# A streaming RWKV-7 and latent-attention layer: the chunk stage with one 64x64 step matrix per chunk and batched products

## The reference

```python
def step(S, inp):                     # S: (heads, 64 values, 64 keys)
    r_t, w_t, k_t, v_t, kk_t, a_t = inp
    sa = jnp.einsum('bhvk,bhk->bhv', S, kk_t)
    S = (S * w_t[:, :, None, :] + v_t[..., None] * k_t[:, :, None, :]
         - sa[..., None] * (kk_t * a_t)[:, :, None, :])
    return S, jnp.einsum('bhvk,bhk->bhv', S, r_t)
```

## Time and profile before

| | |
|---|---|
| time, median of 3 runs | 2530.11 us (2524.06 to 2531.42) |
| the profiled execution's own time | 2529.77 us |
| its span | 2528.1 us |
| mean granted TensorE clock | 0.988 |
| TensorE busy, of the span | 2453.5 us, 97% |
| TensorE weight loads | 2245.9 us, 89% |
| VectorE | 1140.8 us, 45% |
| ScalarE | 861.8 us, 34% |
| GpSimd | 108.6 us, 4% |
| DMA moved | 284.10 MB, mean 112 GB/s |

### The profile page before, as it was taken

One profiled execution on the slowest core, in us unless ns is written; L12 is line 12 of the kernel. 1 busy time (PEld: TensorE's weight loads), 2 busy tenths in 40 slices (PEclk: granted clock), 3 DMA queues, 4 the chain that ended last, 5 costly groups with the idle time before them and its releaser, 6 DMA issues.

```text
span 2528.1 us, 43507 instructions
## 1 busy us (share of the span) xinstructions
PE 2453.5 (97%) x17004; PEld 2245.9 (89%) x17004; DVE 1140.8 (45%) x1840; ACT 861.8 (34%) x1295; POOL 108.6 (4%) x182
## 2 busy tenths in 40 slices
PE   6999999999999999999999899999999999999997
PEld 6888888888889999999978899999878999999886
DVE  4566665665433333344433544444332444444234
ACT  4433333333333322344323433333222333333232
POOL 4000000000010000000000000000000000000010
PEclk9999999999999999999999999999999999999999
DMA  5322222222443433244544344444444444444443
GB/s 161 106 74 72 66 69 70 79 74 73 116 118 108 117 93 99 86 123 126 166 125 125 92 126 129 127 124 124 125 125 124 125 125 127 129 126 134 136 126 128
DMA packets 414536, 284.10 MB, mean 112 GB/s; under 512 B 31728, under 2 KB 392690, under 8 KB 413536
## 3 DMA queue, kind: packets, MB, share of 16 engines
q1 hardware_dynamic: 405600, 259.16, 35.0%
q0 software_dynamic: 8832, 23.36, 3.3%
HBM read 275.55 MB, written 6.92 MB: 112 GB/s over the span
## 4 chain that ended last, share of the span: by engine, by line
PE 94%; DVE 3%; issue 1%; ACT 1%; DMA 1%; POOL 0%; DVEq 0%; SPq 0%; POOLq 0%; ACTq 0%
PE banks L1419 20%; PE banks L869 19%; PE banks L873 18%; PE banks L870 18%; PE banks L320 2%; PE banks L882 2%; PE banks L883 2%; PE banks L884 2%; PE banks L384 1%; PE banks L1282 1%; PE banks L446 1%; PE banks L1285 1%; PE banks L440 1%; PE banks L1380 1%; PE banks L457 0%
## 5 line engine op out<-in xcount | busy, mean ns | idle before, releaser
L859 DVE TENSOR_TENSOR w_lo<-w_raw,w_hi 128x1024 fp32r<-128x1024 f32 x482 | 590.3, 1225 | 970.5 <-ACT w_hi L854 969.2
L869 PE MATMUL banks<-x_hi,w_hi 128*128 128x384 f32 x2640 | 917.5, 348 | 8.2 <-DVE w_lo L859 8.2
L873 PE MATMUL banks<-x_hi,w_lo 128*128 128x384 f32 x2640 | 887.5, 336 | 0.0
L870 PE MATMUL banks<-x_lo,w_hi 128*128 128x384 f32 x2640 | 886.4, 336 | 0.0
L854 ACT ACTIVATE w_hi<-w_raw 128x1024 fp32r<-128x1024 f32 x482 | 511.3, 1061 | 1042.4 <-PE banks L873 599.4
L869 PEld LDWEIGHTS banks<-x_hi,w_hi 128*128 128x128 f32 x2640 | 498.6, 189 | 29.0 <-DVE w_lo L859 10.1
L870 PEld LDWEIGHTS banks<-x_lo,w_hi 128*128 128x128 f32 x2640 | 498.4, 189 | 4.9 <-issue 0.2
L873 PEld LDWEIGHTS banks<-x_hi,w_lo 128*128 128x128 f32 x2640 | 498.2, 189 | 1.2 <-issue 1.2
L1419 PE MATMUL banks<-w_hi,act_hi 128*128 128x512 f32 x528 | 163.6, 391 | 4.6 <-DVE h_rows L1976 2.4
L1419 PE MATMUL banks<-w_hi,act_lo 128*128 128x512 f32 x528 | 164.2, 392 | 0.0
L1419 PE MATMUL banks<-w_lo,act_hi 128*128 128x512 f32 x528 | 163.8, 392 | 0.0
(11 more groups left out here) (395 smaller groups left out, 2395.1 us busy)
## 6 DMA issues: line engine op xcount, KB each, us to landing
w_raw<-in_w_ffn_in SPq DMA_DIRECT2D x176, 512.0 KB, 3.8
w_raw<-in_w_in SPq DMA_DIRECT2D x144, 512.0 KB, 3.8
w_raw<-in_w_ffn_down SPq DMA_DIRECT2D x88, 512.0 KB, 3.6
w_raw<-in_w_out SPq DMA_DIRECT2D x32, 512.0 KB, 3.6
w_raw<-in_w_o_a SPq DMA_DIRECT2D x16, 512.0 KB, 4.0
w_raw<-in_w_o_b SPq DMA_DIRECT2D x16, 512.0 KB, 3.9
w_raw<-in_w_in SPq DMA_DIRECT2D x20, 256.0 KB, 3.7
w_ukv_head<-in_w_ukv POOLq DMA_DIRECT2D x8, 512.0 KB, 4.0
```

The lines of the kernel that those rows point to most:

```text
L859: nc.vector.tensor_tensor(lo[:, s], raw[:, s], hi[:, s].bitcast(F32), ALU.subtract).then_inc(lo_done, 1)
L869: nc.tensor.matmul(out, hi[:, s, k, :], xh[:, kt, :], start=kt == 0, stop=False)
L870: nc.tensor.matmul(out, hi[:, s, k, :], xl[:, kt, :], start=False, stop=False)
L873: last = nc.tensor.matmul(out, lo[:, s, k, :], xh[:, kt, :], start=False, stop=kt == 15)
```

## The change

r and u of all chunks are made before any state is known, in batches. `m_t` v is taken in level 4, for all chunks and the samples, into bank 7, and ScalarE copies it to `ra[:, 0:3]`. In the front four more products turn alpha to token-major form, `ra[:, 3:5]`. One group then multiplies `t_f` with both (128 columns per product): u without the state, and the decayed alpha matrix; a second set of products makes the latter's transposed form `p_t`. The gain of each chunk's state and a 64x64 matrix per chunk and head (`step_made`, to which VectorE adds the identity: `s_step`) follow for all four chunks together. The states are then stepped three times by `s_step`, one product per head and chunk, added in the bank to the gain; `next_state` scales the sum by two columns at once. Afterwards `p_t` times the incoming states corrects u for all chunks in one subtraction, and the output is summed for two chunks per product (128 columns).

The samples' spread `vx` has four blocks of 64 columns in place of eight; the two halves of the tokens (partitions 0 to 63 and 64 to 127) hold four sequences each, so the update takes four products per source, 64 rows by 64 columns of weights with 256 columns, one in each quarter of the array, and values and u are summed in the bank. One addition to the states is left of two. The constant mask shrinks from 8 to 4 columns.

One piece moves from the run after the third `pieces(2)` into the chunk stage, which has six in place of five.

```diff
@@ constants, tiles
-NC2 = R2 + NT + 8
+NC2 = R2 + NT + 4
...
+        ra = region("r_and_alpha", [P, 5, P])
+        un_s = t_y[:, 0:2, :].rearrange("p i c -> p (i c)")
+        u_and_p = region("u_and_p_neg", [P, 2, 2, P])
+        p_t = region("decayed_alpha_t", [P, 2 * P])
+        s_step = t_x[:, 0:4, :].rearrange("p (h t) c -> p h t c", h=2)
+        s_in = region("state_in", [P, 4, 64])
...
+        state_sum = lambda c, r=slice(0, P): ps[r, 2 + 2 * (c % 2), 64 * (c // 2):64 * (c // 2) + 64]
+        step_made = lambda c, r=slice(0, P): ps[r, 2 + 2 * (c % 2), 128 + 64 * (c // 2):192 + 64 * (c // 2)]
+        by_half = [(t, p, i) for t in range(2) for i in range(2) for p in range(2)]
+        by_parity = [(t, p, i) for t in range(2) for p in range(2) for i in range(2)]
@@ pe_rwkv, front
+            for t in range(2):
+                for i in range(2):
+                    last = mm_(ps[:, 2 + i, 384 + 64 * t:448 + 64 * t], al[heads(i), i, tile_tok(t)],
+                               ident[heads(i), heads(i)], start=True, stop=True)
             last.then_inc(E("tok_ps"), 1)
@@ pe_rwkv, levels
                 last.then_inc(E("g_ps"), 1)
+                if lv == 4:
+                    for t, p, i in by_half:
+                        mm_(ps[heads(p), 7, 128 * t + 64 * i:128 * t + 64 * i + 64], m_t[heads(p), 3 * i + t, heads(p)],
+                            v[heads(p), t, heads(i)], start=True, stop=True)
+                    mm_(ps[:, 7, 256:384], asd[:, :], ident, start=True, stop=False, skip_group_check=True)
+                    for i in range(2):
+                        last = mm_(ps[:, 7, 256 + 64 * i:320 + 64 * i], m_t[:, 3 * i + 2, :], v[:, 2, heads(i)],
+                                   start=False, stop=True, skip_group_check=True)
+                    last.then_inc(E("r_ps"), 1)
                 pieces(1, level_ready)
...
+                if b == 6:
+                    pe.wait_ge(E("r_done"), f + 1)
@@ pe_rwkv, chunk stage (the loop over c goes)
+            pe.wait_ge(E("c_done"), f * 2 + 2)
+            wp = ps[:, 2, :].rearrange("p (t q c) -> p t q c", t=2, q=2)
+            for t, p, i in by_half:
+                last = mm_(wp[heads(p), t, :, heads(i)], t_f[heads(p), 3 * i + t, heads(p)], ra[heads(p), t:t + 4:3, heads(i)],
+                           start=True, stop=True)
+            last.then_inc(E("u_ps"), 1)
+            for i in range(2):
+                last = mm_(ps[:, 3, heads(i)], t_f[:, 3 * i + 2, :], ra[:, 2, heads(i)], start=True, stop=True)
+            last.then_inc(E("u_ps"), 1)
+            for t, p, i in by_parity:
+                last = mm_(ps[heads(i), 6 + p, 64 * t:64 * t + 64], ra[heads(p), 3 + t, heads(i)],
+                           t_f[heads(p), 3 * i + t, heads(p)], start=True, stop=True)
+            last.then_inc(E("u_ps"), 1)
+            pieces(1)
+            pe.wait_ge(E("u_done"), f * 2 + 2)
+            pe.wait_ge(E("pa_done"), f + 1)
+            for t, p, i in by_parity:
+                r = heads(p)
+                mm_(state_sum(2 * t + p, heads(i)), tok[r, 0, t, heads(i)], v[r, t, heads(i)],
+                    start=t == 0, stop=False, skip_group_check=True)
+            for t, p, i in by_parity:
+                r = heads(p)
+                mm_(state_sum(2 * t + p, heads(i)), tok[r, 1, t, heads(i)], u_and_p[r, t, 0, heads(i)],
+                    start=False, stop=True, skip_group_check=True)
+            for t, p, i in by_parity:
+                r = heads(p)
+                last = mm_(step_made(2 * t + p, heads(i)), u_and_p[r, t, 1, heads(i)], tok[r, 1, t, heads(i)],
+                           start=False, stop=True, skip_group_check=True)
+            last.then_inc(E("state_ps"), 1)
...
+            pieces(1)
+            for c in range(1, 4):
+                pe.wait_ge(E("state_done"), f * 4 + c)
                 for i in range(2):
+                    last = mm_(state_sum(c, heads(i)), s_step[heads(i), c % 2, c // 2, :], s_in[heads(i), c, :],
+                               start=False, stop=True, skip_group_check=True)
                 last.then_inc(E("state_ps"), 1)
+                if c < 3:
                     pe.wait_ge(E("vx_done"), f * 2 + c)
                     for i in range(2):
+                        for r in range(2):
+                            last = mm_(ps[heads(i), 6 + r, 0:256], tok[heads(r), c - 1, 2, heads(i)],
+                                       vx[heads(r), i].rearrange("p b v -> p (b v)"), start=c == 1, stop=c == 2)
                     last.then_inc(E("sd_ps"), 1)
+                    pieces(1)
+            for t, p, i in by_parity:
+                last = mm_(ps[heads(p), 2 + i, 256 + 64 * t:320 + 64 * t], p_t[heads(i), 128 * t + 64 * p:128 * t + 64 * p + 64],
+                           s_in[heads(i), 2 * t + p, :], start=True, stop=True)
+            last.then_inc(E("us_ps"), 1)
...
+            pieces(1)
+            pe.wait_ge(E("us_done"), f + 1)
...
             pieces(1)
...
-            pieces(4)
+            pieces(3)
@@ act_rwkv
+            fn(ra[:, 3:5, :].rearrange("p t (i c) -> p i t c", i=2),
+               ps[:, 2:4, 384:512].rearrange("p i (t c) -> p i t c", t=2), ACT.Copy).then_inc(E("alpha_done"), 1)
             cut(0)
...
+            act.wait_ge(E("r_ps"), f + 1)
+            fn(ra[:, 0:3, :], ps[:, 7, 0:NT], ACT.Copy).then_inc(E("r_done"), 1)
             cut(3)
...
+            act.wait_ge(E("u_ps"), f * 3 + 1)
+            fn(u_and_p[:, :, :, :].rearrange("p t q c -> p (t q c)"), ps[:, 2, :], ACT.Copy, scale=-1.0).then_inc(E("u_done"), 1)
+            act.wait_ge(E("u_ps"), f * 3 + 2)
+            fn(un_s[:, :], ps[:, 3, 0:P], ACT.Copy, scale=-1.0).then_inc(E("u_done"), 1)
@@ dve_rwkv, chunk stage
+            def next_state(c):
+                return nc.vector.tensor_scalar(s_in[:, c + 1, :], state_sum(c), e1[:, 64 * c + 63:64 * c + 64],
+                                               emid[:, c + 1, 0:1], M, M)
+            dve.wait_ge(E("u_ps"), f * 3 + 3)
+            cp(p_t[:, :].rearrange("p (t h c) -> p h t c", t=2, h=2),
+               ps[:, 6:8, 0:128].rearrange("p h (t c) -> p h t c", t=2)).then_inc(E("pa_done"), 1)
+            dve.wait_ge(E("tok_done"), f + 1)
+            by_sequence(tok[:, 2, 2, :])
+            if more:
+                dve_scan(f + 1, ch)
+            dve.wait_ge(E("state_ps"), f * 4 + 1)
+            next_state(0)
+            tt(s_step[:, :, :, :], each(fold["ident"], 2),
+               ps[:, 2:5:2, 128:256].rearrange("p h (t c) -> p h t c", t=2), A).then_inc(E("state_done"), 1)
+            if more:
+                dve_centre(ch)
+                dve_excl()
+            dve.wait_ge(E("state_ps"), f * 4 + 2)
+            next_state(1).then_inc(E("state_done"), 1)
+            dve.wait_ge(E("u_done"), f * 2 + 2)
+            dve.wait_ge(E("sd_ps"), f * 2 + 1)
+            by_sequence(un_s[:, :])
+            dve.wait_ge(E("state_ps"), f * 4 + 3)
+            next_state(2).then_inc(E("state_done"), 1)
+            cut(4)
+            dve.wait_ge(E("yd_ps"), f + 1)
+            dve.wait_ge(E("us_ps"), f + 1)
+            u_all = u_and_p[:, :, 0, :].rearrange("p t (i d) -> p i t d", i=2)
+            tt(u_all, u_all, ps[:, 2:4, 256:384].rearrange("p i (t d) -> p i t d", t=2), S).then_inc(E("us_done"), 1)
+            dve.wait_ge(E("state_ps"), f * 4 + 4)
+            nc.vector.tensor_scalar(st[:, :], state_sum(3), e1[:, 255:256], None, M).then_inc(E("state_done"), 1)
             dve.wait_ge(E("sd_ps"), f * 2 + 2)
+            s0h = s0t[:, :, :].rearrange("p (r b) v -> p r (b v)", r=2)
+            link(tt(s0h, s0h, ps[:, 6:8, 0:256], A))
```

More of the change, by code:

```diff
@@ L89, in constants @@
     reset = np.broadcast_to(1 - first.astype(f), (P, NT))
-    bm = (s // 16 == np.arange(8)[None]).astype(f)
+    bm = (s % 64 // 16 == np.arange(4)[None]).astype(f)
     half = 32
@@ L187, in build @@
         db = region("proj_diff", [P, 3, PAD])
-        vx = at("v_by_sequence", [P, 2, NB, 64], db_off)
+        vx = at("v_by_sequence", [P, 2, 4, 64], db_off)
         z = region("z", [P, 3, NT])
@@ L214, in build @@
         so = region("s_out", [64, NB, P])
-        st = region("state", [P, 3, 64])
+        st = region("state", [P, 64])
         sto = region("state_rows", [64, P])
@@ L393, in pe_rwkv @@
             for t in range(3):
-                last = transpose(ps[:, 4, t * P:t * P + P], z[:, 2, t * P:t * P + P])
+                transpose(ps[:, 4, t * P:t * P + P], z[:, 2, t * P:t * P + P])
+            for t in range(2):
+                for i in range(2):
+                    last = mm_(ps[:, 2 + i, 384 + 64 * t:448 + 64 * t], al[heads(i), i, tile_tok(t)],
+                               ident[heads(i), heads(i)], start=True, stop=True)
             last.then_inc(E("tok_ps"), 1)
@@ L416, in pe_rwkv, with first_ready @@
             last.then_inc(E("mt_ps"), 1)
-            pieces(1, lambda: pe.wait_ge(E("t_first_done"), f + 1))
+            v = tok[:, 2]
```

(46 more changed lines are left out.)

117 lines of the change are left out of this document (6 added, 111 removed).

## The result

The changed kernel took 2499.57 us, the median of four runs (2493.42 to 2501.7); the kernel before, beside it, 2527.15 (2524.06 to 2531.42). The ratio is 0.9884 (95% interval 0.9869 to 0.9898), 27.6 us less. The profiled execution took 2497.85 us, its span 2496.2, at a mean granted clock of 0.989.

A forecast was written before the change was run, and what follows sets the result against it. TensorE, 94% of the chain, bounds the kernel. Per pass 4.8 + 1.04 - 0.5 - 1.25 = 4.1 us; 7 x 4.1 + 3.4 = 32, so 2530 - 32 = 2498 us, range 2490 to 2512.

The forecast's parts named there:

- the stage: Chunk stage, first chunk product to group-norm mean: 14.6 us on TensorE in place of 19.40, 7.33 small work plus six pieces.
- the first: First group of the new stage: eight diagonal products 0.95, samples' two u products 0.59, eight quarter products 0.28; 1.82 us.
- sums and the samples' output: In the stage: 24 quarter products for state sums and step matrices, plus the unchanged samples' output; 2.35 us.
- three steps with their updates: In the stage: three state steps at 0.17 us each, two samples' updates at 0.5 each; 1.51 us.
- the output's products: End of the stage: four with v 0.49 us, six with the states 0.34, four with u 0.49.
- The six pieces: Projection pieces in the stage: five at 1.23 us between small groups, the last 1.14; 7.3 us together.
- the front's alpha products: Four products added in the front, outside the stage: 0.5 us a pass, bounds 0.28 to 0.63.
- the block of level 4: Added in level 4: eight diagonal products 0.5 us, the samples' asd product and two m_t products 0.75.
- The fourth rival: Quarter products don't run beside each other in the stage: net 2.9 us a pass slower, 2553 us; chance 0.05.
- the third: Rival: quarter groups start less densely, 46 ns a record not 17.5, 2.3 us more a pass, 2516 us; chance 0.07.
- The covers: VectorE and ScalarE work is done before TensorE asks, so it costs nothing; closest the second spread, 0.6 us.
- rival on waits: Late VectorE makes steps and correction wait 1 to 2 us a pass, 2506 to 2514, chance 0.14; pass-head wait, chance 0.05.

The follow-up runs named there:

- the run of the same quarter twice running: Changed kernel with its two diagonal groups ordered to set one array quarter twice in succession; ratio 0.9879 to the kernel before, a pass of 65.75 us.
- the late VectorE: Changed kernel with two extra VectorE operations, read by nothing, ahead of the second spread; median 2506.85 us, ratio 0.9913, a pass of 66.73 us.
- The kernel with the sum on VectorE: Changed kernel, two pieces moved behind the mean, own tile per spread, level 4's samples' alpha-state product dropped and added by VectorE; median 2498.82 us.
- the one with two spreads: Changed kernel with the two pieces behind the updates moved behind the mean and a tile of its own for each spread; median 2494.7 us, ratio 0.9874.
- the one with three pieces out: Changed kernel, own tile per spread, three stage pieces moved behind the mean, two VectorE operations moved behind the third state; 2493.89 us, ratio 0.9867.

## Why the prediction was right

It gave 2498 us; the two medians of the changed kernel are 2499.57 and 2503.78. The mechanism held in each step: TensorE's work and waits in the stage set the pass, the waits went, and none came in their place. The size was a little off: 32 us forecast, 27.6 and 25.2 (2528.98 less 2503.78) between medians, 28 by the passes. That 2498 came so near owes something to the base: I took 2530, and the kernel before measured 2527.15 beside the changed one.

- *The stage:* 14.6 forecast, 15.19. By groups: the first 2.00 (forecast 1.82), sums and the samples' output 2.34 (2.35), three steps with their updates 0.69, 0.70 and, with the correction, 0.50 (1.84 together, and 1.89 measured), the output's products 0.48, 0.45 and 0.59 (1.32, and 1.52 measured). The six pieces, from 1.24 to 1.27 and the last 1.16, took 7.44 (7.3).
- *What was mis-sized* is the edge of a small group. I took prices from groups ahead of neighbours of their own shape: 0.28 for a quarter group, 0.34 for six products by the pair rate. Ahead of such neighbours they came out so (274.22 to 274.50: 0.28; 274.50 to 274.74: 0.24). Where another shape follows, a group costs 0.1 more (that the change of shape is the cause is read from the neighbours; no run changed the shape alone): 0.34 (274.74 to 275.08, ahead of 128x64), 0.39 (from 272.58, ahead of a piece), 0.45 (from 282.72), and 0.59 (from 284.41) where 0.49 was forecast. I had counted it for the first of these and put it elsewhere into the pieces alone. The other three are 0.3 of the 0.6 by which the stage is longer; 0.15 are the pieces, 0.07 the first diagonal group.
- *Added outside:* the front's alpha products 0.60 (0.5), the block of level 4 1.26 (1.25). The net is then 4.21 + 1.04 - 0.60 - 1.26 = 3.4 for pass 3; the pass itself is 3.54 shorter, and the 0.15 between the two was not traced.
- *The new quarter products:* a step with its update takes 0.69 (277.81 to 278.50), against 0.67 forecast; the accumulating groups are as dense as the others. The fourth rival (quarters one after the other) and the third are out, and the run of the same quarter twice running says why the third was never likely.
- *The covers,* the time left when TensorE asks: the first state had 1.9 us (forecast 1.7), the second spread 0.31 to 0.46 (0.6), the correction 1.5 (1.4). In the front VectorE ends its triangle 0.48 us before the piece's last matmul (forecast 0.15), at the head of the pass 1.8 as forecast. No rival on waits came true; the late VectorE, whose pass pays 1.07 of the 1.44 us that reach the spread, puts the spread's true margin near 0.37.

The Trainium skill ("TensorE: Matmul & The Clock Gate", section "Wait — 56ns, not 53.3ns?") has matmuls start no closer than about 25 ns; the group at 274.50 starts 16 records in 0.24 us, 15 ns each, so by this trace the floor doesn't hold for products in different quarters. The Trainium skill's "TensorEngine Tiling (Array Packing)", section "Key Properties", says that a change of tiling mode drains the engine; the 0.1 us that the last group ahead of another shape pays fits that, and no run here shows a drain as such.

## What to carry to other kernels

Price a group of small products by its neighbours as well: each change of the array's shape cost about 0.1 us on both sides here, as much as three 64x64 products. A shorter product is worth its time only where nothing else waits under it; a batch that takes the latency off the chain first (2.0 us a pass) is what made the shorter update (1.1) pay in full. And measure a loop by the distance of its passes: in two profiles of the changed kernel it repeated to 0.01 us, where that kernel's whole runs lay up to 12.6 us apart (2493.42 to 2506.01).

## What the hardware showed that I had not expected

The same changed kernel took 2497.85 us in one profiled execution and 2506.01 in another, with passes equal to 0.01 us. The difference lies in short stretches outside the passes at a lower granted clock. Table by stretches, the changed kernel, first profile:

```profile
30.00:40.00 10.00, 8.67 (x55) 8.48 (x56) 3.21 (x6) 3.37 (x17) 0.98 (x2) 1.00 0.57 147
...
1220.00:1240.00 20.00, 16.98 (x72) 14.02 (x72) 7.69 (x10) 4.49 (x6) 1.61 (x3) 0.91 0.67 245
...
1740.00:1760.00 20.00, 17.79 (x83) 14.80 (x82) 7.07 (x8) 4.81 (x6) 0.00 (x0) 1.00 0.33 109
2300.00:2310.00 10.00, 10.00 (x46) 8.20 (x45) 2.45 (x2) 3.03 (x3) 4.17 (x8) 1.00 0.65 211
```

The same kernel, profiled again:

```profile
30.00:40.00 10.00, 8.84 (x47) 8.65 (x48) 2.24 (x2) 1.80 (x15) 0.79 (x2) 0.83 0.57 147
...
1220.00:1240.00 20.00, 16.97 (x68) 14.16 (x67) 7.36 (x10) 5.17 (x6) 1.60 (x3) 0.83 0.69 260
...
1740.00:1760.00 20.00, 17.79 (x79) 15.15 (x78) 7.28 (x13) 5.08 (x6) 0.00 (x0) 0.91 0.33 105
2300.00:2310.00 10.00, 8.09 (x36) 6.69 (x35) 2.59 (x5) 1.47 (x2) 0.53 (x1) 0.83 0.59 200
```

From 30 to 40 us the one runs at 1.00, the 2.4 GHz level, the other at a mean of 0.83, part of it at 1.2 GHz (from 31.66 to 34.54 its matmuls start 0.32 us apart, where they start 0.17 apart at 1.00), and its first chunk stage starts 1.39 us later. In both, TensorE had been idle for 2.2 us just before, for a weight split of VectorE, so the rows don't tell why the clock fell in one alone. From the start of the last chunk stage to the end they differ by 6.8 us (1897.3 and 1904.1), with three more such stretches above. Summed over stretches of 10 us up to 2480, what the clock is short of 1.00 comes to 22.1 us in the first profile, 30.6 in the second and 25.5 in that of the kernel before; taken as time lost, that is an estimate. So of the 31.9 us between the first two profiles of this document some 3.4 are clock; 28.5 are left, what the passes say. The kernel with the sum on VectorE was at 30.6 too, the one with two spreads and the one with three pieces out at 22.2. For the first two of these that covers the 6.0 us by which the spans of the two go the other way than their passes.
